# 184 groups of mixer steps of a three-block transformer kernel take another place among the weight slots, by a table

## The chip, the core and the metric

The kernel runs on one core of a Trainium2 chip. The metric is the device time of one execution in microseconds (us), the median of three runs. The engines are named as in the profile: PE is TensorE (matmuls) and PEld its weight loads, DVE is VectorE, ACT is ScalarE, POOL is GpSimd, and SP is the engine that issues the DMAs.

## What is computed

Three blocks follow each other on one sequence of 256 tokens of 2048 numbers, in fp32. The first joins an RWKV-7 mixer and a chunked attention, the second a top-k sparse attention and a spatial gate, the third a pooling mixer and a dilated attention; the second and third end in a squared-relu MLP.

```python
def first_block(x, ...):
    h = _rms_norm(x, pre_norm_g)
    p_r, p_k, p_v, z_r, q_a, k_a_att, v_a, z_a, m_r, m_a = split(h @ w_in)
    y_r = _rwkv7_mixer(h, p_r, p_k, p_v, ...) * silu(z_r)
    y_a = _chunk_band_attention(q_a, k_a_att, v_a, rel_bias) * silu(z_a)
    merged = (sigmoid(m_r + b_merge[0]) * (y_r @ w_branch_rwkv)
              + sigmoid(m_a + b_merge[1]) * (y_a @ w_branch_attn))
    return x + _rms_norm(merged @ w_out, post_norm_g)

def second_block(x, ...):
    q, k, v, qi, ki, wi, u_s, v_s, ga, gb = split(rms_norm(x, norm1_g) @ w_in)
    attn = sparse_attention(q, k, v, qi, ki, wi, rel_bias)
    sgu = spatial_gating(gelu(u_s), gelu(v_s), sgu_ln_g, sgu_ln_b, sgu_w, sgu_b)
    x = x + (sigmoid(ga) * attn + sigmoid(gb) * sgu) @ w_out
    x = x + square(relu(rms_norm(x, norm2_g) @ w_ff1)) @ w_ff2
    return rms_norm(x, final_g)

def third_block(x, ...):
    u, q, k, v = split(rmsnorm(x, norm_mix_g) @ w_in)
    y_pool = rmsnorm(pool_mixer(u, pool_w, pool_scale), pool_out_norm_g)
    y_attn = rmsnorm(dilated_attention(q, k, v, slopes), attn_out_norm_g)
    x = x + concatenate([y_pool, y_attn]) @ w_out
    x = x + square(relu(rmsnorm(x, norm_mlp_g) @ w_up)) @ w_down
    return rmsnorm(x, norm_final_g)
```

## The kernel before

**The weight stream.** All large products run in one stream of 1084 slots. A slot is eight blocks of 128 weight rows by 128 columns. For each pair of slots SP loads 1 MB into a ring of three (`load_unit`, L2419). For each slot ACT copies the weights to a rounded high half (`split_high`, L2429), DVE subtracts it to get the low half (`split_low`, L2436), and PE multiplies: eight matmuls of the high half with the token operand's two halves (128x512, L2526) and eight of the low half (128x256, L2530), all into a sums buffer `gp`. The splits run two slots ahead of PE, in four slots' worth of `w_parts`. When a block of columns ends, its sums are read out by ACT (L2037), DVE (L2139, L2143, L2177) and in some sections POOL (L2081).

The sections follow each other in this order, with the first slot of each: `qkv` 0, `za` 48, `rkv` 64, `gates` 112, `zr` 176, `branch` 192, `out` 224 (block 1); `index2` 256, `qkv2` 268, `v2` 316, `u2` 348, `ga2` 380, `gb2` 412, `out2` 444, `up2_0` 476, `down2_0` 540, `up2_1` 604, `down2_1` 668 (block 2); `in3` 732, `out3p` 796, `out3a` 812, `up3_0` 828, `down3_0` 892, `up3_1` 956, `down3_1` 1020 (block 3, to 1084).

**The steps beside it.** Everything else (the mixers, attentions, norms, tables) is written as "threads". A `Thread` has a start place, counted in slots, a pace, and one generator for each engine that works for it; each `yield tick` gives the place `start + tick * pace` of what follows. A `Beside` object on each engine's instruction stream runs the steps whose place has been reached. PE asks it at the start of a slot (q), after half of the high products (q + 0.34) and after all of them (q + 0.67); ACT and DVE ask at the same three places, `side.run(q)` standing ahead of the slot's `split_high` or `split_low`, the other two behind it and around the read-out of a block. The engines run in order, so a step whose inputs are late holds back whatever stands behind it on its engine. Data and waits are fixed by semaphores; only the order on each engine follows from the places.

**Names that the prediction uses.** Threads `rwkv_0` and `rwkv_1` work each on four groups of heads, one after another (0 to 3), beside `gates` and `zr`. Of one group: `norms` (DVE L963 and L965 give `kk_squared`, PE L1115 sums it over a head: `headones`), `norm_spread` (after the root chain on DVE, L969 then L90 to L95, then L975; PE L1115 with `ident,smalls`), `cumulated` (DVE L997 sigmoid, PE L1115 with `consts`, then three exponentials on ACT, L1082 to L1084), `ab`/`ak` (DVE L1004 to L1009 `r_hat`, `z_hat`, `b_hat`, `k_hat`, then PE L1115 64x128), and at the group's end `mean`, `var`, the same root chain and `var_spread` (L1055, L90 to L95, then PE and DVE L1062). All PE steps of these threads go through one helper, L1115. Threads `att2_0`, `att2_1` (beside `qkv2` to `gb2`) and `att3_0`, `att3_1` (beside `in3`) are attentions: DVE stages v, k and q (L1293, L1294, L1299, into `low`), PE transposes v (L1348) and makes logits (L1354, L1355), ACT copies (L1329), and later PE transposes the probabilities (L1361). `sgu_0`/`sgu_1` are the spatial gate (DVE L1660, PE L1692). `pool` is the pooling mixer beside `in3` (its last DVE step is L1809), `tables3` makes distance tables beside `up2_0` (DVE L1737 to L1744), `start` and `lora` stand at the beginning (norms of x: PE L419 waits for a DVE root chain ending in L95), and `post` between `out` and `index2`.

Of the kernel before, what the change touches and what calls it, by code (L numbers as in the profile page):

```python
# [34 lines left out]
FAR, TAKEN = -1.0e38, -3.0e38  # L35


class Section:


    def __init__(self, name, blocks, nk, source, wide=False):
        self.name, self.blocks, self.nk, self.source, self.wide = name, blocks, nk, source, wide
        self.chunks = SLOT // 2 if wide else SLOT
        self.slots = nk // self.chunks
        self.slot0 = self.block0 = 0
# [14 lines left out]
class Beside:  # L60


    def __init__(self, eng, key, threads):
        self.live = []
        for t in threads:
            if key in t.programs:
                g = t.programs[key](eng)
                self.live.append([t, g, next(g, None)])

    def run(self, place):  # L70
        for entry in self.live:
            t, g, tick = entry
            while tick is not None and t.start + tick * t.pace <= place + 1e-9:
                tick = next(g, None)
            entry[2] = tick


class InverseRoot:
# [2530 lines left out]
```

## Time and profile before

| | us |
|---|---|
| median of three runs | 3455.51 (3454.36 to 3463.07) |
| span of the profiled execution | 3455.6 |
| PE busy | 3366.9 (97%) |
| PE weight loads busy | 2908.9 (84%) |
| DVE busy | 2204.8 (64%) |
| ACT busy | 1543.8 (45%) |
| POOL busy | 295.2 (9%) |

The span runs from the first to the last instruction of the profiled execution, which is the only one for which a trace exists; it is within 0.1 us of the median of the three. PE busy is the share of the span in which a matmul was in work, the weight loads overlap it, and a busy PE is not PE at its full rate: the same matmul takes about twice as long where the granted clock is at its lower level.

### The profile page before, as it was taken

How to read it: one execution, taken by the hardware profiler on the slowest of the kernel's cores; microseconds unless marked ns; L12 is line 12 of the kernel's file. 1: busy time of each engine (PE TensorE's matmuls, PEld its weight loads, DVE VectorE, ACT ScalarE, POOL GpSimd, SP SyncE). 2: the span in 40 equal slices, each digit the busy share in tenths (PEclk: the TensorE clock that was granted, in tenths of full speed). 3: DMA queues.
4: the chain of work that ended last, by engine and by line, in shares of the span. 5: the costliest groups of instructions: out<-in, count | busy, mean ns of one | idle time of the engine just before them, and what ended most of it. 6: DMA issues, size and time to landing. Idle time of an engine off the chain costs nothing.

```text
span 3455.6 us, 52015 instructions
## 1 busy us (share of the span) xinstructions
PE 3366.9 (97%) x21718; PEld 2908.9 (84%) x21718; DVE 2204.8 (64%) x3040; ACT 1543.8 (45%) x2121; POOL 295.2 (9%) x318
## 2 busy tenths in 40 slices
PE   8999999999989999999999999999999999999998
PEld 7888877778878888888888888888888888888887
DVE  5567655556667576777666446655777866446654
ACT  4454433334543455544544334444454544334443
POOL 3100122220011111100100000001000100000000
PEclk9999999999989999999999999999999999999999
DMA  6554433335535545655555656555544556556554
GB/s 193 180 178 151 138 111 116 107 107 195 190 123 171 187 154 169 193 164 173 182 193 186 193 185 192 187 191 188 166 159 159 183 184 207 194 183 195 192 198 146
DMA packets 550751, 592.98 MB, mean 172 GB/s; under 512 B 16757, under 2 KB 511733, under 8 KB 550262
## 3 DMA queue, kind: packets, MB, share of 16 engines
q1 hardware_dynamic: 550518, 589.66, 52.7%
q8 instruction: 172, 2.82, 0.3%
q14 instruction: 61, 0.50, 0.0%
HBM read 583.24 MB, written 6.32 MB: 171 GB/s over the span
## 4 chain that ended last, share of the span: by engine, by line
PE 87%; DVE 7%; ACT 2%; issue 2%; DMA 1%; POOL 0%; SPq 0%; DVEq 0%; ACTq 0%; POOLq 0%
PE gp L2526 45%; PE gp L2530 24%; PE gp L2511 7%; PE sidep L1115 4%; PE gp L2516 3%; DVE w_parts L2436 2%; ACT w_parts L2429 1%; DVE stage L2143 0%; DMA high<-bias_rows 0%; PE sidep L570 0%; ACT lo_half L2037 0%; PE sidep L1355 0%; DVE stage L2139 0%; DMA ring<-w_branch_rwkv 0%; DVE low L2175 0%
## 5 line engine op out<-in xcount | busy, mean ns | idle before, releaser
L2436 DVE TENSOR_TENSOR w_parts<-ring,w_parts 128x1024 fp32r<-128x1024 f32 x1084 | 1368.9, 1285 | 452.8 <-ACT w_parts L2429 451.5
L2526 PE MATMUL gp<-x_parts,w_parts 128*128 128x512 f32 x5840 | 1481.7, 398 | 11.1 <-issue 5.5
L2429 ACT ACTIVATE w_parts<-ring 128x1024 fp32r<-128x1024 f32 x1084 | 1109.8, 1053 | 453.5 <-PE gp L2516 188.9
L2526 PEld LDWEIGHTS gp<-x_parts,w_parts 128*128 128x128 f32 x5840 | 1061.7, 190 | 215.6 <-issue 13.4
L2530 PEld LDWEIGHTS gp<-x_parts,w_parts 128*128 128x128 f32 x5840 | 771.8, 191 | 48.0 <-issue 6.7
L2530 PE MATMUL gp<-x_parts,w_parts 128*128 128x256 f32 x5840 | 801.4, 285 | 2.8 <-DVE w_parts L2436 2.6
L2037 ACT ACTIVATE lo_half<-gp 128x512 f32<-128x512 f32 x239 | 142.8, 598 | 892.1 <-PE gp L2526 459.4
L2526 PE MATMUL gp<-ff_parts,w_parts 128*128 128x512 f32 x1792 | 430.8, 391 | 0.0
L2526 PEld LDWEIGHTS gp<-ff_parts,w_parts 128*128 128x128 f32 x1792 | 328.6, 188 | 63.0
L2139 DVE TENSOR_TENSOR stage<-gp,lo_half 128x512 f32<-128x512 f32 x168 | 116.2, 692 | 377.3 <-ACT lo_half L2037 376.4
L2511 PE MATMUL gp<-w_parts,ff_parts 128*128 128x512 f32 x1024 | 273.7, 389 | 0.0
L2530 PEld LDWEIGHTS gp<-ff_parts,w_parts 128*128 128x128 f32 x1792 | 230.9, 191 | 10.6 <-issue 1.4
L2530 PE MATMUL gp<-ff_parts,w_parts 128*128 128x256 f32 x1792 | 235.4, 283 | 0.3 <-DVE w_parts L2436 0.3
L2511 PEld LDWEIGHTS gp<-w_parts,ff_parts 128*128 128x128 f32 x1024 | 192.3, 188 | 39.9
L538 POOL TENSOR_TENSOR low<-low 128x512 f32<-128x512 f32 (+1 forms) x38 | 59.0, 1558 | 1237.0 <-ACT low L529 648.9
L2516 PE MATMUL gp<-w_parts,ff_parts 128*128 128x512 f32 x512 | 157.5, 389 | 0.0
L2139 DVE TENSOR_TENSOR high<-gp,lo_half 128x512 f32<-128x512 f32 x63 | 43.5, 691 | 165.8 <-ACT lo_half L2037 165.7
L2053 ACT ACTIVATE ff_parts<-stage 128x512 fp32r<-128x512 f32 x64 | 40.5, 632 | 166.8 <-DVE stage L2177 166.8
L2516 PEld LDWEIGHTS gp<-w_parts,ff_parts 128*128 128x128 f32 x512 | 96.1, 188 | 19.9
L2081 POOL TENSOR_TENSOR high<-high,rstd 128x512 f32<-128x512 f32 x40 | 57.5, 1437 | 458.5 <-DVE high L2139 440.7
L1115 PEld LDWEIGHTS sidep<-high 64*64 64x64 f32 x1696 | 60.3, 133 | 42.7 <-issue 17.8
L1115 PE MATMUL sidep<-high 64*64 64x64 f32 (+1 forms) x1696 | 73.4, 233 | 16.2 <-DVE high L1007 4.6
(392 smaller groups left out, 1867.1 us busy)
## 6 DMA issues: line engine op xcount, KB each, us to landing
ring<-w_in SPq DMA_DIRECT2D x220, 1024.0 KB, 5.1
ring<-w_ff SPq DMA_DIRECT2D x128, 1024.0 KB, 5.6
ring<-w_up SPq DMA_DIRECT2D x64, 1024.0 KB, 6.0
ring<-w_down SPq DMA_DIRECT2D x64, 1024.0 KB, 5.0
ring<-w_out SPq DMA_DIRECT2D x48, 1024.0 KB, 5.3
ring<-w_branch_attn SPq DMA_DIRECT2D x8, 1024.0 KB, 5.2
ring<-w_branch_rwkv SPq DMA_DIRECT2D x8, 1024.0 KB, 5.2
gate_scratch<-stage SPq DMA_DIRECT2D x16, 256.0 KB, 2.2
```

The costliest lines, as they stand in the source:

```text
L538: m = pool.tensor_tensor(self.acc[k], self.acc[k], self.sq[b - 1][k], ALU.add)
L1115: return pe.matmul(out, lhs, rhs, start=start, stop=stop, skip_group_check=True)
L2037: act.activation(lo_half[:, k % 2], gp[:, k % 2, :, 1, :], ACT.Copy).then_inc(lo_copied, 1)
L2053: act.activation(ff_parts[:, 2 * b:2 * b + 2, 0, :], st, ACT.Copy).then_inc(ff_high_split, 1)
L2081: pool.tensor_tensor(to, to, over(rstd, 2), ALU.mult).then_inc(scaled_by_pool, 1)
L2139: v.tensor_tensor(to, gp[:, k % 2, :, 0, :], lo_half[:, k % 2], ALU.add).then_inc(block_evacuated, 1)
L2429: act.activation(w_parts[:, q % PARTS, 0], ring[:, u % RING, SLOT * (q % 2):SLOT * (q % 2) + SLOT, :], ACT.Copy).then_inc(high_split, 1)
L2436: v.tensor_tensor(w_parts[:, q % PARTS, 1], ring[:, u % RING, SLOT * (q % 2):SLOT * (q % 2) + SLOT, :], w_parts[:, q % PARTS, 0].bitcast(F ...
L2511: pe.matmul(wide_sums(k, t), operand(s, b, s.chunks * n + c)[:, half, tokens], w[:, 0, c, :], start=(n == 0 and c == 0 and half == 0), sto ...
L2516: m = pe.matmul(wide_sums(k, t), operand(s, b, s.chunks * n + c)[:, 0, tokens], w[:, 1, c, :], start=False, stop=(n == s.slots - 1 and c = ...
L2526: return pe.matmul(gp[:, k % 2, j, :, :], w_parts[:, q % PARTS, 0, c, j * P:(j + 1) * P], operand(s, b, SLOT * n + c), start=(n == 0 and c ...
L2530: return pe.matmul(gp[:, k % 2, j, 0, :], w_parts[:, q % PARTS, 1, c, j * P:(j + 1) * P], operand(s, b, SLOT * n + c)[:, 0, :], start=Fals ...
```

## The change

A table `MOVED` gives, for a thread and an engine, the number of slots that are added to the place of its n-th step (counted from 0); `Beside` adds it when it asks whether a step has been reached. Most steps have no entry and stay. The table has 185 entries: 105 on PE, 64 on VectorE, 15 on ScalarE (these are the 184 of the title) and one on SyncE, a load of a table; 105 make the step later, 80 earlier. No instruction, wait or buffer is added or taken away. Line numbers after the table are 58 higher in the changed kernel (L1115 is L1173 there).

```diff
+MOVED = {
+    ("att2_0", "tensor"): {0: 1.12, 1: 0.57, 7: 0.7, 13: 1.29, 14: 1.07, 20: 0.87},
...
+    ("att3_1", "vector"): {0: -0.16, 14: -0.5},
...
+    ("pool", "vector"): {15: 1.17},
...
+    ("rwkv_0", "tensor"): {0: 1.72, 1: 0.88, 30: 0.35, 31: -0.1, 32: -0.05, 35: -0.18, 38: -0.2, 39: -0.09, 40: -0.32,
+        42: -0.1, 49: -0.36, 50: -0.58, 51: -0.48, 55: -0.05, 56: -0.28, 61: 0.42, 62: 1.47, 63: 1.63, 66: 0.44,
+        92: -0.01, 115: -0.01, 116: -0.24, 117: -0.46, 121: 1.12},
...
+    ("tables3", "vector"): {0: -2},
...
+}
@@ class Beside
-                self.live.append([t, g, next(g, None)])
+                self.live.append([t, g, next(g, None), 0, MOVED.get((t.name, key), {})])
 
     def run(self, place):
         for entry in self.live:
-            t, g, tick = entry
-            while tick is not None and t.start + tick * t.pace <= place + 1e-9:
-                tick = next(g, None)
-            entry[2] = tick
+            t, g, tick, n, moved = entry
+            while tick is not None and t.start + tick * t.pace + moved.get(n, 0) <= place + 1e-9:
+                tick, n = next(g, None), n + 1
+            entry[2:4] = tick, n
```

What it does to the order is shown at three places. The first is PE at the start of `v2` (block 2), where the two attention threads begin a group: L1348 transposes v, L1354 and L1355 make the logits. Before:

```order
L2530 MATMUL gp<-x_parts,w_parts 128x256 x8
L2526 MATMUL gp<-x_parts,w_parts 128x512 x8
L1348 MATMUL sidep<-ident,low 128x128 x4
L2530 MATMUL gp<-x_parts,w_parts 128x256 x8
L2526 MATMUL gp<-x_parts,w_parts 128x512 x4
L1354 MATMUL sidep<-low 128x128
L1355 MATMUL sidep<-low 128x256
L1354 MATMUL sidep<-low 128x128
L1355 MATMUL sidep<-low 128x256
L2526 MATMUL gp<-x_parts,w_parts 128x512 x4
```

and after, from one slot further on:

```order
L2588 MATMUL gp<-x_parts,w_parts 128x256 x8
L2584 MATMUL gp<-x_parts,w_parts 128x512 x8
L1406 MATMUL sidep<-ident,low 128x128 x2
L1412 MATMUL sidep<-low 128x128
L1413 MATMUL sidep<-low 128x256
L2588 MATMUL gp<-x_parts,w_parts 128x256 x8
L2584 MATMUL gp<-x_parts,w_parts 128x512 x4
L1406 MATMUL sidep<-ident,low 128x128 x2
L2584 MATMUL gp<-x_parts,w_parts 128x512 x4
L1412 MATMUL sidep<-low 128x128
L1413 MATMUL sidep<-low 128x256
```

The transposes moved more than a slot later and the two threads' are apart now; the first thread's logits follow its transposes at once.

The second is DVE beside `in3` (block 3), where the pooling mixer's last step, L1809, stands near the staging of the dilated attention (L1293, L1294, L1299). Before:

```order
L2436 TENSOR_TENSOR w_parts<-ring,w_parts 128x1024
L2143 TENSOR_TENSOR high<-high,rstd 128x512
L1809 SCALAR_TENSOR_TENSOR ff_parts<-high,prm,ff_parts 128x256 x8
L594 COPY variance_t<-sidep 128x256
L1293 TENSOR_SCALAR low<-high 128x256
L1294 TENSOR_SCALAR low<-high 128x256
L1299 TENSOR_SCALAR low<-high 128x256
L2436 TENSOR_TENSOR w_parts<-ring,w_parts 128x1024
```

and after:

```order
L652 COPY variance_t<-sidep 128x256
L1351 TENSOR_SCALAR low<-high 128x256
L1352 TENSOR_SCALAR low<-high 128x256
L1357 TENSOR_SCALAR low<-high 128x256
L2494 TENSOR_TENSOR w_parts<-ring,w_parts 128x1024
L1351 TENSOR_SCALAR low<-high 128x256
L1352 TENSOR_SCALAR low<-high 128x256
L1357 TENSOR_SCALAR low<-high 128x256
L1867 SCALAR_TENSOR_TENSOR ff_parts<-high,prm,ff_parts 128x256 x8
```

The eight instructions of L1809 (L1867 now) stand behind the staging of both attention threads instead of ahead of it.

The third is PE beside `gates` (block 1), about slot 154, where the third group of the RWKV heads gets its running sums (`consts,high` is thread 0, `consts,low` thread 1) and then its `ab`/`ak` products (64x128, both threads). Before:

```order
L1115 MATMUL sidep<-consts,high 128x256 x2
L1115 MATMUL sidep<-consts,low 128x256 x2
L2526 MATMUL gp<-x_parts,w_parts 128x512 x4
L2530 MATMUL gp<-x_parts,w_parts 128x256 x8
L2526 MATMUL gp<-x_parts,w_parts 128x512 x8
L1115 MATMUL sidep<-high 64x128 x32
```

and after:

```order
L1173 MATMUL sidep<-consts,low 128x256 x2
L2584 MATMUL gp<-x_parts,w_parts 128x512 x4
L1173 MATMUL sidep<-consts,high 128x256 x2
L1173 MATMUL sidep<-high 64x128 x32
L2588 MATMUL gp<-x_parts,w_parts 128x256 x8
```

The sums of thread 0 moved about a slot later, and now stand directly ahead of the products that need what ACT and DVE make of them. In the other groups (0, 1 and 3) the sums moved later by a third to a half of a slot, and of group 3 the `ab`/`ak` products too.

## Rows read from the trace of the kernel before

**Rows 1.** The page: its busy times, and the chain that ended last.

```profile
PE 3366.9 (97%) x21718; PEld 2908.9 (84%) x21718; DVE 2204.8 (64%) x3040; ACT 1543.8 (45%) x2121; POOL 295.2 (9%) x318
...
PE 87%; DVE 7%; ACT 2%; issue 2%; DMA 1%; POOL 0%; SPq 0%; DVEq 0%; ACTq 0%; POOLq 0%
```

**Rows 2.** PE by stretches: from:to us, length, busy (xcount), granted clock, DMA share, GB/s.

```profile
391.70:741.70 350.00, 327.32 (x4326) 1.00 0.34 111
741.70:818.10 76.40, 70.29 (x831) 0.98 0.32 104
...
1009.60:1052.80 43.20, 39.99 (x197) 0.82 0.23 64
...
1198.70:1313.80 115.10, 109.20 (x635) 0.97 0.53 167
...
1888.20:2423.90 535.70, 535.70 (x3073) 1.00 0.60 190
```

**Rows 3.** PE's waits, whole span: waiting line, awaited line: us in total, times, longest.

```profile
PE sidep L1348 <- DVE low L1293: 7.0, 5, 2.4
...
PE sidep L419 <- DVE smalls L95: 5.9, 3, 2.6
...
PE sidep L1115 <- DVE high L997: 5.5, 4, 1.6
PE sidep L1115 <- DVE high L1007: 4.6, 2, 3.4
...
PE sidep L1115 <- DVE high L965: 3.4, 2, 2.5
PE sidep L1692 <- DVE low L1660: 3.1, 5, 1.2
...
PE sidep L1354 <- DVE low L1299: 2.5, 2, 1.3
...
PE sidep L1361 <- DVE low L1314: 2.4, 4, 1.0
```

**Rows 4.** Timeline, end of `gates`, group 3: start, duration, engine, line, operation [idle before].

```profile
712.63 1.30 PE L2530 MATMUL gp<-x_parts,w_parts 128*128 128x256 f32 x8
...
714.46 0.47 ACT L1082 ACTIVATE high<-sidep,consts 128x256 f32<-128x256 f32 x1
...
715.60 1.11 PE L2530 MATMUL gp<-x_parts,w_parts 128*128 128x256 f32 x8
...
719.67 0.42 DVE L1007 TENSOR_TENSOR high<-high 128x256 f32<-128x256 f32 x1
...
720.14 1.09 PE L1115 MATMUL sidep<-high 64*64 64x128 f32 x16 [3.43 <-DVE high L1007]
```

**Rows 5.** Timeline, a root chain at the start of `gates`: its first and last instruction.

```profile
400.51 0.22 DVE L969 TENSOR_SCALAR smalls<-sidep 128x4 f32<-128x4 f32 x2
...
404.44 0.17 DVE L975 TENSOR_SCALAR smalls<-smalls 128x8 f32<-128x8 f32 x1
```

**Rows 6.** Timeline, `zr`: PE's spread step behind a root chain.

```profile
807.02 1.97 PE L1115 MATMUL sidep<-ident,smalls 128*64 128x128 f32 x16 [2.37 <-DVE smalls L95]
```

**Rows 7.** Timeline, start of `v2`: the first thread's transposes.

```profile
1211.07 0.44 PE L1348 MATMUL sidep<-ident,low 128*128 128x128 f32 x2 [1.97 <-DVE low L1293]
```

**Rows 8.** Timeline, `in3`: the pooling mixer's last step, and the transposes behind it.

```profile
2522.09 3.26 DVE L1809 SCALAR_TENSOR_TENSOR ff_parts<-high,prm,ff_parts 128x256 fp32r<-128x256 f32 x8
...
2526.06 0.44 PE L1348 MATMUL sidep<-ident,low 128*128 128x128 f32 x2 [2.37 <-DVE low L1293]
```

**Rows 9.** Timeline, `up2_0`: the table chain's first instruction, and PE behind it.

```profile
1735.61 0.29 DVE L1737 CAST consts<-variance_t 128x256 f32<-128x256 int32 x1
...
1740.65 1.18 PE L2530 MATMUL gp<-x_parts,w_parts 128*128 128x256 f32 x8 [2.19 <-DVE w_parts L2436]
```

**Rows 10.** PE behind the waits of Rows 4 and 7, columns as in Rows 2.

```profile
720.10:741.70 21.60, 21.56 (x405) 1.00 0.30 100
...
1213.20:1216.60 3.40, 3.40 (x14) 0.50 0.37 92
```

More of the change, by code:

```diff
@@ L35 @@
 FAR, TAKEN = -1.0e38, -3.0e38
+MOVED = {
+    ("aout_rms", "tensor"): {1: 0.67},
+    ("att1_0", "tensor"): {2: 1.24, 4: 1.2, 5: 1.17, 8: 1.04, 14: 0.5, 16: 0.47},
+    ("att1_1", "tensor"): {2: 1.24, 5: 1.17, 8: 1.04, 14: 1.5},
+    ("att2_0", "scalar"): {5: 0.72},
+    ("att2_0", "tensor"): {0: 1.12, 1: 0.57, 7: 0.7, 13: 1.29, 14: 1.07, 20: 0.87},
+    ("att2_0", "vector"): {2: -0.3, 9: 0.82, 16: 1.17},
+    ("att2_1", "scalar"): {9: 0.74},
+    ("att2_1", "sync"): {1: -0.5},
+    ("att2_1", "tensor"): {0: 1.79, 1: 1.57, 2: 0.39, 6: 0.35, 7: 0.37, 13: 0.95, 14: 0.74, 15: 0.55, 20: 0.54},
+    ("att2_1", "vector"): {8: -0.08, 24: -0.25},
+    ("att3_0", "tensor"): {2: 0.47},
+    ("att3_1", "tensor"): {2: 0.97, 6: 0.64, 10: 1.3, 11: 0.44},
+    ("att3_1", "vector"): {0: -0.16, 14: -0.5},
+    ("bias2", "vector"): {0: 0.84},
+    ("gelu_u", "scalar"): {0: 1.66},
+    ("lora", "tensor"): {1: 0.84, 2: 0.67},
+    ("lora", "vector"): {5: 0.34, 6: 0.5},
+    ("merged", "scalar"): {0: 1},
+    ("merged", "vector"): {0: 1},
+    ("mlp3", "tensor"): {0: 0.33, 1: 0.34},
+    ("mlp3", "vector"): {1: -0.66},
+    ("norm1", "tensor"): {0: 1.33, 1: 2},
+    ("norm2", "tensor"): {0: 0.33, 1: 0.34},
+    ("pool", "vector"): {15: 1.17},
+    ("post", "scalar"): {1: 1.34, 2: 2.66, 3: 2.33},
+    ("post", "vector"): {1: -0.34},
[13 rows of a table added]
+    ("select", "vector"): {15: 0.67, 16: 1.17, 17: 3},
+    ("sgu", "scalar"): {2: 0.79, 3: 1.12},
+    ("sgu", "tensor"): {1: 2.17, 2: 0.67},
+    ("sgu", "vector"): {9: 0.67, 10: 0.79},
[4 rows of a table added]
+    ("start", "tensor"): {5: -1.33, 6: -0.33, 7: -0.67, 8: -1, 9: -2.36},
+    ("start", "vector"): {5: -1.02, 6: -1, 7: 0.68},
+    ("tables3", "vector"): {0: -2},
+    ("y_a", "vector"): {0: -0.67},
+    ("y_r", "scalar"): {1: 1},
+    ("y_r", "vector"): {1: 1.33},
+    ("ya", "scalar"): {6: -1},
+}
 class Section:
```

14 rows, old and new, of the table MOVED are left out of this document.

## The prediction, made before the changed kernel was run

> **What bounds the kernel now.** I read the page first. PE is busy for 3366.9 us of 3455.6, and the chain that ended last is PE for 87% [rows 1]. So PE's stream sets the end, and an edit is worth only what it takes from PE: idle time, time at the lower clock, or matmuls that run slowly. The reader should see next that the busy share flatters PE: on the same page the weight loads are busy for 84% only. The Trainium skill says so too (Perfetto Trace Analysis, "Identifying the Most-Contended Engine"): matmul busy time is a poor measure and the weight loads a better one. The sum below doesn't use that; it goes by waits.
>
> Second, PE by stretches. PE idles 3455.6 - 3366.9 = 88.7 us. The MLP of block 2 has none: 535.70 us of 535.70 [rows 2], and at 16 matmuls a slot its 3073 are 192 slots, so a slot is 2.79 us of PE. `gates` has 350.00 - 327.32 = 22.7, `zr` 6.1, the index section 3.2, `v2` 5.9 [rows 2]: it sits where mixer steps lie in the stream. The largest piece I know of outside the table's reach is the transition to block 2 around `post` and the load of x at the start; together with the tail they are about half of the 88.7.
>
> Third, the waits, by what PE stood for [rows 3]. All the large ones have one form: a mixer step on PE reached before DVE had its operand ready. There a later place for PE's step costs nothing and takes the wait away, since weight products of later slots are ready in between. Fourth, the clock: 3.40 us at a granted clock of 0.50 [rows 10] is the lower of its two levels (1.2 instead of 2.4 GHz), so it does 1.7 us of work and loses 1.7. There are nine places with such stretches; the shown one begins 2.1 us after the end of a wait of 1.97 [rows 7].
>
> **The change, part by part.** Nothing is added or removed, so the only terms are waits that go, waits that come, the clock behind them, and detours: each time PE leaves the stream and returns, the first group of weight products takes 1.30 us instead of 1.11 [rows 4], so 0.19 each.
>
> *Start and `lora`.* PE's L419 waited 2.6 of its 5.9 us here for the root chain [rows 3]; its step is put 2.7 slots later. The transposes of x are pulled into the time in which PE waits for the first split anyway. Together 2.6 and an estimated 1.4 from the transposes: **4.0**.
>
> *`gates`, what goes.* The running sums (waiting for L997) are later in groups 0, 1 and 3, and in group 2 for one thread: 5.5 us [rows 3]. The `ab`/`ak` products of group 3 move on by 1.3 to 1.6 slots, that is at least 3.6 us of stream, against a wait of 3.43 [rows 4]; the shorter wait for L1007 goes too except for a few tenths, 4.2 of 4.6 [rows 3]. Of the other 22.7 - 5.5 - 4.6 - 3.4 = 9.2 us, which are waits of 0.4 to 1.9 for level products, states and sums, the table moves PE's side later or DVE's side earlier at about half: 4.9.
>
> *`gates`, what comes.* (a) Group 0's norm sums are later by 1.5 slots, so the 3.4 us for L965 go [rows 3]. But the spread of the roots now has the same place, and stands directly behind the second sum. It needs the root chain, 404.44 + 0.17 - 400.51 = 4.1 us [rows 5], or some 2.4 without POOL beside it, by PE's wait of 2.37 for most of such a chain in `zr` [rows 6]. PE will wait about 3.1 there: net +0.3. (b) In group 2 the sums of thread 0 are directly ahead of the products made from them. Between stand three exponentials and three DVE operations, 3 x 0.47 + 3 x 0.42 = 2.7 [rows 4], and no weight product: a new wait of 2.7. (c) The spread of group 0's deviations is earlier by a half slot or so than its chain: 1.1. Sum for `gates`: 5.5 + 4.2 + 4.9 + 0.3 - 2.7 - 1.1 = **11**.
>
> *`zr`.* All idle time there is waits of this form, 2.37 of it for one root chain [rows 6]. That spread is later by 1.1 slots, more than 3 us. A stretch at the lower clock follows it at once. 6.1 + 1.7, less seven detours more (1.3): **6.5**.
>
> *The attentions and the spatial gate, `v2` to `gb2`.* L1348 waited 7.0 us, 2.37 of it in `in3` [rows 3, 8], so 4.6 here; L1354 2.5 and L1692 3.1 [rows 3]. L1348 is later by 1.12 slots and 1.79 slots for the two threads, 3.1 us and more against 1.97 [rows 7]; for L1692 PE's steps are later by 0.5 to 1. Two stretches at the lower clock stand behind the L1348 waits: 2 x 1.7. Together 10.2 + 3.4, and 0.9 of smaller waits: **14.5**.
>
> *Index section.* Its wait for the second half of the operand is 2.9 of its 3.2 idle [rows 2]; a `post` step on DVE is earlier by a third and ACT's are later, out of the way: **2.0**, an estimate between 0 and 2.9.
>
> *`up2_0`.* The table chain begins at 1735.61, and PE waits 2.19 for the split behind it, until 1740.65 [rows 9]; less about 1.2 for that split the chain is some 3.8 us of DVE. It goes two slots back, behind that slot's splits. What is late next is the split after it, which is two slots ahead of PE (5.6 us) against 3.8 of chain: covered. **2.2**.
>
> *`in3`, `out3p`.* L1809 is 3.26 us of DVE ahead of the staging for which PE waited 2.37 [rows 8]. Behind both stagings it delays one `split_low` only, which is two slots early. So 2.4, one lower clock stretch 1.7, L1361's 2.4 [rows 3] and 0.9 for the norm there (L419): **7.4**.
>
> *The rest* (`rkv`, `branch`, `qkv2`, `up3_0`): **1.7**.
>
> Gross 4.0 + 11 + 6.5 + 14.5 + 2.0 + 2.2 + 7.4 + 1.7 = 49.3. Against it: PE has 15 detours more, of which I counted seven, 8 x 0.19 = 1.5. And waits that the trace of before can't show, since a step that moves brings its followers to an edge: I set one of 0.5 us for each of 11 later steps that are at a following step's place, 5.5; the bounds are nothing and 1.5 us each (the middle of the waits above), 16. The sum is 49.3 - 1.5 - 5.5 = 42, on 3455.5: **3413**. The profiled execution's 3455.6 and the median 3455.51 agree, so no scaling.
>
> **Does the clock come back?** The sum takes back four slow stretches (one in `zr`, two behind L1348, one in `in3`), 4 x 1.7 = 6.8 us. It is the least sure term: after a wait of 3.43 [rows 4] the granted clock is 1.00 for the 21.6 us behind it, while after 1.97 [rows 7] it falls [rows 10]. A fifth, at the start of `gates`, I leave where it is, since the wait there stays. The Trainium skill's rule (TensorE: Matmul & The Clock Gate, "HAM oscillation") has it that a kernel whose PE pauses for its operands is given the lower clock for the work behind. By that the pauses' end ends these stretches, 6.8 us; if they come regardless of the pauses, the sum is 35 and the time 3420.
>
> **The rivals.**
> 1. *The waits come back elsewhere.* The root chains and exponentials are as long as before; if PE reaches the following step too early, half of what was saved returns, as I found at (a), (b) and (c), where 7 of 21 us return. At half, 21 us are left: 3435. For it: in `gates` almost every step has a follower within a slot or two. Against it: in `v2` and `in3` a group's steps are spread wide.
> 2. *All that is named goes, new waits don't come,* and (a) to (c) are shorter than worked out (PE reaches them later, and DVE is ahead): 49.3 + 7 = 56: 3399.
> 3. *Slower: a DVE side step blocks a split.* 45 or so of the 64 VectorE entries are earlier. One whose input isn't there holds DVE, and with it `split_low` behind it. It costs what [rows 9] shows, 2.19 us, once the hold exceeds the two slots' lead (5.6 us less the split, 1.2). To turn 42 us of gain into no change it takes 42 / 2.2, about 19 such places; at 25 it is 3468. It speaks against it that DVE has 36% of the span free, and that the earlier ones move by a quarter to a half slot (0.7 to 1.4 us), less than the lead.
> 4. *It doesn't do what it says:* steps are reached only at three places a slot, so an entry may round to the old place. The order shows otherwise on PE (three places in the section on the change). Then 3455.
>
> **How the numbers follow.** The forecast 0.63 (own range 3404 to 3424), rival 1 0.17, rival 2 0.11, rival 3 0.05, rival 4 0.04. The predicted time is the forecast's, 3413. Its bounds from the unseen waits are 49.3 - 1.5 - 16 = 32 and 48, so 3424 and 3408; the clock term adds 7 above. The range has to take in most of rivals 1 and 2: 3396 to 3437. A measurement of this kernel can tell about 0.3%, 10 us, from no change: faster means below 3445. Faster: the forecast, rival 2 and all but a little of rival 1, 0.90. Within 0.3%: rival 4 and what is left of rival 1 and the small end of rival 3, 0.06. Slower: 0.04.
>
> **What would show it.** PE idle from 88.7 to about 50. In `gates` from 22.7 to about 12; two waits of PE's L1173 of about 3 us remain or are new there, one at its start for a root chain (its spread), one about slot 154 for L1065. No wait of 2 us at the start of `v2`, in `in3`, in `zr`, nor behind the table chain in `up2_0`, and full clock behind each. The MLPs take the same 535.7. It would be wrong if waits of `w_parts` L2494 appear at PE (rival 3), or if PE's idle time falls while its busy time rises by as much, which would be detours dearer than 0.19 or matmuls slowed otherwise.

## The result, and the profile after

The changed kernel took 3396.92 us (3396.3 to 3398.74, four runs) against 3457.82 for the kernel before (3454.36 to 3463.07), a ratio of 0.9821 with a 95% interval of 0.9807 to 0.9835. It is faster by 60.9 us where 42 were forecast. On the kernel before's 3455.5, from which the prediction was worked out, the ratio gives 3393.7, below the stated range that began at 3396 (the 3396.92 itself lies just inside it, but beside a kernel before of 3457.82). So the direction was right and the size too small by a third.

The page of the changed kernel (span 3394.6 us), the lines that answer to [rows 1]:

```profile
PE 3350.2 (99%) x21718; PEld 2901.7 (85%) x21718; DVE 2199.1 (65%) x3040; ACT 1541.8 (45%) x2121; POOL 305.4 (9%) x318
...
PE 95%; DVE 3%; issue 1%; DMA 0%; POOL 0%; ACT 0%; SPq 0%; DVEq 0%; ACTq 0%; POOLq 0%
```

VectorE's part of the chain that ended last fell from 7% to 3%. PE idles 3394.6 - 3350.2 = 44.4 us, 44.3 less than before. But its busy time fell as well, by 16.7, for the same 21718 matmuls, where the prediction took 6.8 off for the clock and added 2.8 for detours. PE by stretches, as [rows 2] (`gates`, `zr`, index section, `v2`, the MLP of block 2):

```profile
385.00:721.50 336.50, 328.54 (x4325) 0.98 0.35 115
721.50:791.50 70.00, 69.70 (x833) 1.00 0.35 114
...
982.50:1022.00 39.50, 36.76 (x196) 0.90 0.24 67
...
1168.00:1271.30 103.30, 103.30 (x625) 1.00 0.58 182
...
1838.00:2373.70 535.70, 535.70 (x3074) 1.00 0.60 190
```

`v2` has no idle time left (5.9 us before), `zr` 0.3 of 6.1, `gates` 8.0 of 22.7. The MLP is the same to 0.1 us. Of the waits of [rows 3] those for L1293, L997, L965, L1660, L1299 and L1314 are gone altogether. Apart from the first 20 us and from DMA and split waits, the largest for a VectorE step that are left are these; L1173 is the L1115 of before, L1033 its L975, L1065 its L1007, L153 its L95:

```profile
PE sidep L1173 <- DVE smalls L1033: 4.1, 1, 4.1
PE sidep L1173 <- DVE high L1065: 2.4, 1, 2.4
PE sidep L477 <- DVE smalls L153: 2.4, 1, 2.4
...
PE sidep L1173 <- DVE smalls L153: 1.1, 1, 1.1
```

The first, second and fourth are the prediction's (a), (b) and (c): 3.1, 2.7 and 1.1 us forecast. The third is at the transition to block 2, where it is 2.4 before as well. Two waits are new at the very start: 1.9 for a load of x, in place of 2.7 for the first split, and 0.7 for L748.

In us, stage by stage. "Clock" is half the change of the time spent at a granted clock of 0.5 (the last 540 us, equally long in both, are left out of it); the last column is what neither idle time nor clock explains:

| stage | forecast | measured | idle | clock | rest |
|---|---|---|---|---|---|
| start, `qkv` | -4.0 | -3.6 | -2.9 | -0.9 | +0.2 |
| `rkv`, `branch`, `qkv2`, `up3_0` | -1.7 | -4.0 | -1.6 | 0 | -2.4 |
| `gates` | -11 | -13.5 | -14.7 | +3.4 | -2.2 |
| `zr` | -6.5 | -6.4 | -5.8 | -1.7 | +1.1 |
| index section | -2.0 | -3.7 | -0.5 | -3.9 | +0.7 |
| `v2` to `gb2` | -14.5 | -17.4 | -11.3 | -3.4 | -2.6 |
| `up2_0` | -2.2 | -2.4 | -2.2 | 0 | -0.2 |
| `in3`, `out3p` | -7.4 | -10.2 | -5.7 | -3.4 | -1.1 |
| whole span | -42 | -61.0 | -44.3 | -9.4 | -7.3 |

(The forecast's total has 7 us taken off for detours and unseen waits; its stages add up to 49.)

The clock of the first row is not what the clock records alone give. They begin at 18.5 us in the kernel before and at 10.9 in the changed one, and a stretch without a record counts as full clock. The kernel before's first weight products, then the changed kernel's:

```profile
13.37 2.04 PE L2526 MATMUL gp<-x_parts,w_parts 128*128 128x512 f32 x4 [2.66 <-ACT w_parts L2429]
...
15.92 2.05 PE L2526 MATMUL gp<-x_parts,w_parts 128*128 128x512 f32 x4
```

```profile
13.25 1.17 PE L2584 MATMUL gp<-x_parts,w_parts 128*128 128x512 f32 x4
```

The first take nearly twice as long for the same work, so the 5.1 us from 13.4 to 18.5 are counted as the lower level here, against the 3.4 recorded in the changed kernel. That is an inference from the durations.

### The profile page after: what moved, and what is told of

Its sections match the earlier page's. It is cut to its first block, busy times and chain, and to the rows that moved or that the text cites. A ratio compares the mean times of both kernels' runs of the same rounds, so it can differ in the third digit from the quotient of the medians.

```text
span 3394.6 us, 52013 instructions
## 1 busy us (share of the span) xinstructions
PE 3350.2 (99%) x21718; PEld 2901.7 (85%) x21718; DVE 2199.1 (65%) x3040; ACT 1541.8 (45%) x2121; POOL 305.4 (9%) x318
## 4 chain that ended last, share of the span: by engine, by line
PE 95%; DVE 3%; issue 1%; DMA 0%; POOL 0%; ACT 0%; SPq 0%; DVEq 0%; ACTq 0%; POOLq 0%
PE gp L2584 50%; PE gp L2588 26%; PE gp L2569 7%; PE sidep L1173 4%; PE gp L2574 3%; DVE w_parts L2494 1%; PE sidep L1413 0%; PE sidep L628 0%; PE sidep L1498 0%; PE sidep L1419 0%; POOL high L596 0%; PE sidep L1757 0%; PE sidep L900 0%; PE sidep L1879 0%; PE sidep L764 0%
## 5 line engine op out<-in xcount | busy, mean ns | idle before, releaser
L2584 PEld LDWEIGHTS gp<-x_parts,w_parts 128*128 128x128 f32 x5840 | 1058.4, 189 | 211.2 <-issue 10.9
L2588 PEld LDWEIGHTS gp<-ff_parts,w_parts 128*128 128x128 f32 x1792 | 230.9, 191 | 10.9 <-issue 1.8
L1173 PEld LDWEIGHTS sidep<-high 64*64 64x64 f32 x1696 | 60.5, 133 | 30.1 <-issue 17.9
L2139 POOL TENSOR_TENSOR stage<-stage,rstd 128x512 f32<-128x512 f32 x32 | 49.6, 1549 | 350.0 <-DVE stage L2197 350.0
```

The lines of the kernel that those rows point to most:

```text
L1173: return pe.matmul(out, lhs, rhs, start=start, stop=stop, skip_group_check=True)
L2139: pool.tensor_tensor(to, to, over(rstd, 2), ALU.mult).then_inc(scaled_by_pool, 1)
L2584: return pe.matmul(gp[:, k % 2, j, :, :], w_parts[:, q % PARTS, 0, c, j * P:(j + 1) * P], operand(s, b, SLOT * n + c), start=(n == 0 and c ...
L2588: return pe.matmul(gp[:, k % 2, j, 0, :], w_parts[:, q % PARTS, 1, c, j * P:(j + 1) * P], operand(s, b, SLOT * n + c)[:, 0, :], start=Fals ...
```

## What a wait costs beside PE's idle time

A source of the last column stands in the timeline. Two places of the same step, the three transposes L1361 in `in3`; first the kernel before, where PE waited for VectorE:

```profile
2541.02 1.10 PE L2530 MATMUL gp<-x_parts,w_parts 128*128 128x256 f32 x8
...
2542.16 0.35 DVE L1314 TENSOR_SCALAR low<-low,smalls 128x256 f32<-128x256 f32 x1
...
2542.56 0.31 PEld L1361 LDWEIGHTS sidep<-ident,low 128*128 128x128 f32 x3 [0.64 <-DVE low L1314]
2542.56 0.55 PE L1361 MATMUL sidep<-ident,low 128*128 128x128 f32 x3 [0.44 <-DVE low L1314]
...
2542.86 1.41 PE L2526 MATMUL gp<-x_parts,w_parts 128*128 128x512 f32 x5
```

and the changed kernel, where the operand is ready (L1419 is L1361):

```profile
2523.22 1.09 PE L2584 MATMUL gp<-x_parts,w_parts 128*128 128x512 f32 x4
...
2523.41 0.35 DVE L1372 TENSOR_SCALAR low<-low,smalls 128x256 f32<-128x256 f32 x1
...
2523.92 0.48 PEld L1419 LDWEIGHTS sidep<-ident,low 128*128 128x128 f32 x3
2524.15 0.49 PE L1419 MATMUL sidep<-ident,low 128*128 128x128 f32 x3
...
2524.40 1.17 PE L2584 MATMUL gp<-x_parts,w_parts 128*128 128x512 f32 x4
```

Without a wait the weight load begins 0.23 us ahead of its first matmul, beneath the matmul before it. With a wait both begin at once. Count from the moment at which the stream's next product could have begun, one product's interval (0.12 us for 256 columns, 0.23 for 512) behind the start of the last: the detour takes 0.90 us with the wait and 0.25 without, 0.65 for 0.44 of idle time. The same reading at other waits of the kernel before whose step has one form: L1348 in `in3` 2.58 for 2.37, L1692 five times 0.21 to 0.23 more than its idle time, L1354 1.54 for 1.26, L419 2.81 for 2.57. So each of these waits costs PE's idle entry and another 0.21 to 0.28 us. It isn't so for every wait: L1440, which waits for a DMA, costs 0.03 more.

Where the 0.21 of L1361 lies can be read from the single records. The last product starts at 2541.84 and its modelled end is 2542.12, so the idle entry begins 0.16 behind 2541.96, when the next could have started: matmuls in a row overlap, and the entry leaves that out. The other 0.05 is the first transpose, 0.33 us instead of the 0.27 of the next, with its load now ahead of it. Whether the other waits divide in this way was not read.

A test without the clock: e9 below leaves block 2 as it was, and has no lower clock in `v2` and `u2`, like the changed kernel. They take 215.6 us there and 206.4 in the changed kernel. Of the 9.2 us 7.5 are idle time; the other 1.7 come with seven waits, 0.24 each.

PE's list of waits has 57 before and 18 now. 39 x 0.25 is 9.8, an estimate that is above the 7.3 of the last column; the 15 detours more can be the difference, and so can the halving of the slow time, which is too much in `zr` and the index section, where the last column is positive. Neither is shown. The rows on which the prediction stood hinted at the price: [rows 7, 8] are PE's entries, and the idle entry of PEld is nearer to it, 0.64 for 0.65 at L1361 and 2.79 for 2.58 at L1348.

## Experiments

All but the three shifted ones are the table with other entries; the line numbers of an experiment are up to 51 above those of before. e5 to e11 and e14 ran once each: they are read stage by stage, from their traces, and not by their totals.

### Which side of the table does it?

The first takes PE's entries alone, the second all others.

```diff
 MOVED = {
     ("att1_0", "tensor"): {...},
-    ("att2_0", "scalar"): {...},
-    ("att2_0", "vector"): {...},
...
```

> The changed kernel with only the 105 PE entries of the table; VectorE, ScalarE and SyncE keep their places. Theory A (the gain of about 61 us is PE reaching its mixer steps later, when their operands are ready): at least 50 of the 61 us come, about 3400 to 3408; missing are the L1809 wait in in3 (2.4 and a slow stretch), the table chain in up2_0 (2.2) and the index section (3.7). Theory B (the two sides have to be shifted together; a DVE step at its old place ahead of a split now waits for a PE step that is later, and holds the split): less than 35 us come, 3420 or more, and PE waits for w_parts L2494.

Measured: 3454.76 us (3450.54 to 3456.6), ratio 0.9984 (0.9974 to 0.9993). Theory A, which is also the prediction's, falls: 4 us, not 50. PE in `gates`, then its waits there:

```profile
386.90:755.60 368.70, 339.25 (x4326) 0.96 0.32 105
```

```profile
PE sidep L1136 <- DVE high L1028: 7.0, 3, 3.4
PE sidep L1136 <- DVE high L1054: 4.3, 2, 3.7
PE sidep L1136 <- DVE smalls L996: 3.9, 1, 3.9
PE sidep L1136 <- DVE high L1018: 3.4, 3, 1.5
PE sidep L1136 <- DVE high L1000: 3.2, 1, 3.2
```

`gates` is 368.7 us long instead of 350.0: PE idles 29.5 instead of 22.7 there, and 30.6 us of it run at the lower clock instead of 3.4, which costs 13.7 by halving. `v2` shows the table's other face: it is shorter by 8.8 of the 11.8 us. The total is theory B's, but its sign, waits for the split, is hardly there: PE waits 4.0 us for VectorE's `w_parts` in all, 2.9 before. What PE waits for is the mixer's own operands.

> The changed kernel with only the 80 entries of VectorE, ScalarE and SyncE; PE keeps its places. Theory A: about 8 to 12 us faster than before (in3 4.1, up2_0 2.2, index section 3.7, little in gates), 3444 to 3448. Theory B: the earlier VectorE steps alone shorten many of the waits in gates and zr, 20 us or more in all, 3435 or less.

Measured: 3443.9 (3441.59 to 3444.72), ratio 0.9952 (0.9937 to 0.9967). The two halves give 4 and 15 us, together 19 of the 61. Neither theory: `in3`, `out3p` and `up2_0` gave 9.6 as A had it, and the early steps of VectorE 3.6 in `gates` (6.5 of idle time, half of which the lower clock took back: 10.2 us of it instead of 3.4) and 2.4 in `zr`, as B had it, but new waits came where VectorE's side had been moved later without PE's:

```profile
PE sidep L1382 <- DVE low L1327: 6.0, 3, 3.2
PE sidep L1601 <- DVE low L1627: 4.0, 1, 4.0
PE sidep L1388 <- DVE low L1333: 3.0, 2, 1.5
```

These are L1348 (4.6 before), L1567 (0.8) and L1354 (2.5), between `v2` and `gb2`. In the index section PE waits 4.0 us for POOL's operand, 0.3 before, as in e8 below.

The third leaves out, of PE's entries, the 27 that make a step earlier.

```diff
-    ("rwkv_0", "tensor"): {0: 1.72, 1: 0.88, 30: 0.35, 31: -0.1, 32: -0.05, 35: -0.18, ...
+    ("rwkv_0", "tensor"): {0: 1.72, 1: 0.88, 30: 0.35, 61: 0.42, 62: 1.47, 63: 1.63, 66: 0.44, 121: 1.12},
```

> Of the table only PE's 78 entries that make a step later; its 27 earlier ones and all of VectorE, ScalarE and SyncE are left out. If the earlier PE steps spoiled e1 (they need operands that VectorE makes no earlier), gates has less idle time than the 29.5 us of e1 and of the 22.7 of before: 17 us or less, and the kernel is at 3435 to 3445. If PE's later steps themselves hold VectorE and thereby the next step, gates idles 25 us or more again, and the kernel is at 3450 or above.

Measured: 3443.44 (3440.69 to 3447.75), ratio 0.9955 (0.9939 to 0.9972). The time is the first theory's, the place is not. PE's earlier steps did cost e1 some 10 us (ratios 0.9984 and 0.9955), but in `gates` the later ones by themselves save nothing:

```profile
387.80:744.60 356.80, 333.58 (x4326) 0.98 0.34 109
```

23.2 us of idle time against 22.7, which is neither the 17 or less of the first theory nor the 25 or more of the second; the stage is 6.8 us longer than before by the clock, 17.1 us at the lower level instead of 3.4. Where the waits of the kernel before went, others came: L995 (L975 before) has 3.9, L1027 (L1007) 7.0 in three places instead of 4.6 in two. The reading that fits: a PE step that is later makes what VectorE and ScalarE do with its result later too, and if the following PE step stays, it waits. The table moves both sides.

### The step that the prediction told wrongly

The prediction put the waits of 1.63 and 3.43 us in the last group of heads [rows 4] down to a later place of PE's steps there, and so does the section on the change, in its last sentence. The table has no such entry: in groups 0, 1 and 3 PE's sums stay where they are, behind as many weight products as before (2744 in group 3), and so do the `ab`/`ak` products of group 3. What is moved there is VectorE, and one step of ScalarE.

```diff
+    ("rwkv_0", "vector"): {69: -0.24, 70: -0.46, 71: -1.02, 72: -0.2},
+    ("rwkv_1", "vector"): {69: -0.24, 70: -0.46, 71: -1.02},
+    ("rwkv_0", "scalar"): {43: -0.13},
```

> The kernel before with eight entries only: of group 3 of rwkv_0 and rwkv_1 the VectorE steps sigmoid, kka and hats are earlier by 0.2 to 1.0 slots, one ScalarE step by 0.13; no PE step moves. It tells apart who took away the waits of 1.63 (L997, at 711.0) and 3.43 us (L1007, at 720.1). The prediction put them down to a later PE step; the table has no such entry for group 3. Theory B (VectorE's earlier steps do it): both waits go, the idle time of gates falls from 22.7 to about 17.6. Rival (PE's later steps do it): both stay.

PE's waits in `gates` for the same two lines, L1004 (L997) and L1014 (L1007):

```profile
PE sidep L1122 <- DVE high L1004: 3.9, 3, 1.6
...
PE sidep L1122 <- DVE high L1014: 1.1, 1, 1.1
```

One of four and one of two are gone, 1.6 and 3.5 us; the idle time of `gates` is 346.00 - 328.48 = 17.5. So these eight entries bring the 5 us without any PE step. In the trace VectorE's sigmoid comes earlier and its products stand ahead of a `split_low` (L2436) instead of behind it; and the one ScalarE entry puts the first thread's exponentials (L1082) ahead of a read-out (L2037), 1.07 us behind the start of the sums instead of 3.47. Which of the two the wait for L1007 needed was not taken apart. This is shown for group 3.

### Single places

> The kernel before with nine entries of the table only: PE's transposes and logits (L1348, L1354) of att2_0 and att2_1 at the starts of both groups are later by 0.6 to 1.8 slots. The waits 1.97, 0.92, 0.85 and 0.91 us go, 4.6 us. Theory A (the slow stretches at 1213.2 and 1308.7 come from the pauses ahead of them): they go too, 3.4 us more, so v2 shrinks from 115.1 to 107 or less. Rival (they come from something else, or by chance): both stay, v2 is 110.5.

```diff
+    ("att2_0", "tensor"): {0: 1.12, 1: 0.57, 13: 1.29, 14: 1.07},
+    ("att2_1", "tensor"): {0: 1.79, 1: 1.57, 13: 0.95, 14: 0.74, 15: 0.55},
```

`v2`, as in [rows 2], and what PE still waits for in it:

```profile
1207.90:1316.40 108.50, 104.25 (x625) 1.00 0.53 170
```

```profile
PE sidep L1354 <- DVE low L1299: 1.6, 1, 1.6
PE sidep L1367 <- DVE low L1320: 1.4, 2, 1.0
PE sidep L1360 <- DVE low L1305: 1.3, 1, 1.3
```

115.1 became 108.5. Both stretches at the lower clock are gone from it (0.97 became 1.00), as theory A has it, but that doesn't show theory A: e9, with the same waits in `v2` as before (5.9 us), has neither stretch either and takes 112.0, and e3, e7 and e8, which leave these waits alone, have one. Against e9 the edit gives 3.5 us. Of idle time 1.6 us are gone: the start of the first group no longer waits, while the transposes of the second wait 1.6 at one place instead of 0.85 and 0.91 at two, and the probabilities' transposes (L1367, the L1361 of before) wait 1.4 that wasn't there. The other entries of these threads take those away in the changed kernel. The run as a whole took 3461.36, no less than before, because `gates`, which the edit doesn't touch, was 7.5 us longer. The next section is on that.

> The kernel before with one entry: the pooling mixer's last VectorE step (eight instructions, 3.26 us) is 1.17 slots later, behind the staging of both attention threads. The wait of 2.37 for L1293 goes, and by theory A the slow stretch behind it (1.7): in3 from 213.1 to 209.0. If the held split or the next attention step takes the place of that wait, 211 to 213.

```diff
+    ("pool", "vector"): {15: 1.17},
```

`in3` became 210.4 us, 2.7 less. The wait of 2.37 for the first transposes is gone and another of 1.3 has come, so the idle time fell by 1.0, which is nearer to the rival's case. The other 1.7 are the stretch at the lower clock behind it, and they aren't the edit's: e3, e6, e8 and e9 keep the wait, lack the stretch and take 211.4 or 211.5.

```profile
PE sidep L1353 <- DVE low L1298: 1.3, 1, 1.3
```

> The kernel before with the four entries of the thread post: ScalarE's roundings of x for block 2 (groups 1 to 3) are later by 1.34, 2.66 and 2.33 slots, and a VectorE step is earlier by 0.34. The index section took 43.2 us before and 39.5 in the changed kernel. Theory A: these four entries give at least 3 of the 3.7 us (40.2 or less), with the wait for L2295 shorter. Rival: most of the 3.7 us is a slow stretch less, which comes or goes with the timing of what precedes: 42 or more here.

The index section became 44.7 us, 1.5 longer. Its wait for the operand's second half fell, but the step ahead now waits for POOL:

```profile
PE sidep L576 <- POOL high L544: 2.9, 1, 2.9
PE gp L2532 <- DVE x_parts L2301: 1.8, 2, 0.9
```

In the changed kernel `norm1`'s steps on PE are 1.33 and 2 slots later as well, and that wait is 0.4. Of the 3.7 us there, 3.9 are the clock, and the clock isn't the table's alone: e4 below has the same entries here, 13.3 us at the lower level instead of 8.0, and takes 41.2.

> Only the entries of the threads rwkv_0 and rwkv_1, on all engines (87 of 185). If stages are independent: gates 336.5 us long as in the changed kernel (350.0 before), zr 70.0 (76.4 before), all other stages as before: 19.9 us less, 3436. If what one stage gives the next (DMA prefetch, slow stretches carried over) counts, the sum differs by more than 2 us.

Measured: 3436.97 (3433.29 to 3437.04), ratio 0.9931 (0.9916 to 0.9945). `gates` and `zr`:

```profile
392.00:728.40 336.40, 328.41 (x4325) 0.98 0.35 115
728.40:798.30 69.90, 69.60 (x832) 1.00 0.36 114
```

That is the changed kernel's 336.5 and 70.0. The entries of this mixer work on their own stages and can be tuned by themselves; e1, e2 and e13 show that PE's and the other engines' can't be taken apart within `gates`.

### The price of a detour

```diff
+    ("att1_1", "tensor"): {0: 0.34, 1: 0.34, ...},
```

> The kernel before, with one entry set that the change doesn't have: all 24 PE steps of the thread att1_1 (beside rkv) get 0.34 slots, so that they no longer stand directly behind those of att1_0. PE leaves the weight stream 18 times more. By the prediction's price of 0.19 us per detour the stage rkv grows from 172.6 us by 3.4, less up to 1.4 of waits that a later place removes: 174.6 or more. Rival: a detour costs nothing of its own, since weight products of the stream fill what the step's own chain leaves open: 171.2 to 172.6.

```profile
219.10:393.10 174.00, 172.91 (x994) 1.00 0.48 158
```

The stage took 174.0 us, 1.4 more than before, for 18 detours more; 0.4 us of waits went, so 0.10 each, between the 0.19 expected and the rival's nothing. It hangs on the step: pairs of L834, L841 and L842 took 2.38 us together and 1.17 + 1.16 apart, L858 to L860 1.54 and then 0.89 + 0.90. The prediction's 0.19, read off the longer first group of products behind a detour [rows 4], is thus too dear here. What the 15 more detours cost in the changed kernel can't be told from the price of its waits.

### The clock

Before and the same kernel with a shift:

```diff
                         pe.wait_ge(high_split, q + 1)
+                        for _ in range(4 if s.name == "za" and b == 1 and n == 0 else 0):
+                            high_product(0, 0)
```

> The kernel before with four matmuls more (the first product of a block in za is made five times, each time started anew; 128x512, 0.228 us each), so that everything behind slot 52 comes 0.9 us later and nothing else changes. Theory C (whether a pause brings a slow stretch hangs on when it falls, so the same program has another set of them when it is shifted): gates to in3 show slow stretches at other places than before, and the time differs from before plus 0.9 by several times 1.7 us, up or down. Rival (slow stretches belong to their pauses): the same nine places, each 0.9 later, and 3456.5.

> As e10 with eight matmuls more, a shift of 1.8 us. Theory C: a third set of slow stretches, other than those of before and of e10. Rival: the same places, 1.8 later, and 3457.4.

They took 3465.14 and 3463.34, beside 3460.61 (3454.35 to 3466.3, seven runs) for the kernel before in the same comparison. Four stretches of the kernel with the shift of 0.9 us, in `gates` and `zr`:

```profile
503.80:507.20 3.40, 3.40 (x14) 0.50 0.20 77
677.90:681.30 3.40, 3.40 (x8) 0.51 0.20 77
725.60:729.00 3.40, 3.40 (x38) 0.51 0.17 43
793.90:797.30 3.40, 3.40 (x33) 0.50 0.00 0
```

and the same work in the kernel before, found by counting weight products (0.9, 2.6, 4.3 and 6.0 us earlier, since each slow stretch on the way delays what follows by another 1.7):

```profile
502.90:506.30 3.40, 3.40 (x30) 1.00 0.20 77
675.30:678.70 3.40, 3.40 (x49) 1.00 0.20 77
721.30:724.70 3.40, 3.40 (x52) 1.00 0.18 49
787.90:791.30 3.40, 3.40 (x53) 1.00 0.00 1
```

The waits in `gates` and `zr` are the same, the clock is not: 14 matmuls in place of 30 at the first. `gates` idles 22.7 us in both and takes 354.8 instead of 350.0. Shifted by 1.8, there are slow stretches at 505.2 and 573.4 in `gates`, and one in `branch` at 856.7, with those at 677.9 and 725.6 gone. Theory C holds: the same pause on PE may or may not be followed by one, and a shift of 0.9 us changes which. The seven runs of the kernel before in that comparison show it without a shift; span and mean granted clock:

```
3452.6 us 0.992    3453.7 us 0.992    3457.0 us 0.991    3458.9 us 0.990
3459.7 us 0.990    3459.4 us 0.989    3464.5 us 0.988
```

The profiled execution on which the prediction rests (3455.6 us, 0.992) was among the quick ones. So was its `gates`: of the seven traces in which the table leaves that stage alone (the kernel before, e5 to e8, e10, e11) it idles 22.1 to 22.7 us in all, and takes 350.0 to 357.5, with 3.4 us at the lower clock in the kernel before and 20.5 in e6. The stage table above, which sets one execution against one, is uncertain by as much in its clock column. The same shift on the changed kernel:

> The changed kernel with four matmuls more in za, a shift of 0.9 us as in e10. If slow stretches need pauses, and it has few, its set stays small: 3396.3 + 0.9, within 3.4, and no stretch between slots 120 and 255. If they come by chance regardless of pauses, new ones appear in gates to gb2 and it is 3 to 8 us longer.

It took 3396.24 us, and its span, 3394.5, is the changed kernel's 3394.6: `gates` took 336.1 for 336.5, and the rest of the 0.9 us lies in a few tenths elsewhere. One slow stretch did come within it, at 604.9 behind the wait for L1065, in the place of one at the start of `gates`, so the set isn't fixed (none was expected there), but it stays as small. Outside the transition to block 2 and the last 540 us the four kernels with all or nearly all of the table (the changed one, e4, e12, e14) have 7 to 17 us of recorded lower clock, those of the seven traces above 24 to 44. The changed kernel's four runs lie within 2.4 us, where the kernel before's four had 8.7; but e12's four spread over 6.1, so a small spread isn't shown to be the table's.

### Can the table be bettered?

Each of these alters a few entries at the waits (a), (b) and (c).

```diff
-    ("rwkv_0", "tensor"): {..., 63: 1.63, ...}
+    ("rwkv_0", "tensor"): {..., 63: 1.3, ...}
```

> The changed kernel with one entry altered: in rwkv_0 on PE, step 63 (the running sums of group 2) is later by 1.30 instead of 1.63 slots, so it stands beside that of rwkv_1 and half of a slot's high products lie between it and the ab/ak products. The changed kernel waits 2.42 us there. 0.9 us of matmuls now lie between: the wait falls to about 1.3 and one detour less: 1.1 to 1.5 us faster than the changed kernel, 3395.5, ratio to before 0.9817. Rival: DVE holds the split first and the exponentials come no earlier: no change, 3397.

Measured: 3395.4 (3394.47 to 3395.68), ratio 0.9819 (0.9803 to 0.9835). The wait is 1.2 us instead of 2.4. The second has this, and in both threads on PE `1: 1.22, 2: 0.43, 31: 0.16`:

> The changed kernel with e4's edit and six more entries altered: at the start of gates PE's spread of the norm roots is a third of a slot later (115.34) for both threads and the step behind it another third (115.67); at slot 133 the spread of group 0's deviations is a third later. Half of a slot's products (0.9 us) then lie under each of the waits of 4.06 and 1.05 us: 4.06 falls to 3.1 or less, 1.05 to 0.1 or less. About 1.5 to 1.9 us less than e4 (3395.4): 3393.7, unless the next step waits instead, in which case 3395.4.

Measured: 3394.65 (3390.35 to 3396.45), ratio 0.9809 (0.979 to 0.9828). PE's waits in `gates`:

```profile
PE sidep L1166 <- DVE smalls L1026: 3.0, 1, 3.0
PE sidep L1166 <- DVE high L1058: 1.2, 1, 1.2
PE sidep L1166 <- DVE high L1084: 0.3, 1, 0.3
```

4.1, 2.4 and 1.1 became 3.0, 1.2 and nothing, as expected; that the whole gained 1.5 us or more beyond e4, as was expected too, isn't shown. The medians are 1.5 and 2.3 us below the changed kernel's, but the intervals of the ratios lie over each other: the waits are shown to be shorter, that the kernel is faster is not.

## Why the prediction was right or wrong

- **What bounds the kernel** was right. PE sets the end, the gain is waits in the mixer stages, and the MLPs didn't change.
- **The idle time** came out near what was named: 49.3 gross, without its 6.8 of clock and with the 1.3 taken off for detours in `zr`, is 43.8, and 44.3 were measured. `zr` was right to a tenth in sum; (b) was 2.42 for 2.7, (c) 1.05 for 1.1, (a) 4.06 for 3.1: the root chain took 4.0 us there, with POOL busy beside all of it.
- **"... the only terms are waits that go, waits that come, the clock behind them, and detours": the largest miss.** A wait was priced at PE's idle entry and its further price put at nothing. At the waits that could be read it is 0.21 to 0.28 us more. What neither idle time nor clock explains came out at -7.3 where the forecast, which had only detours there, had +2.8: 10.1 us of the 18.7 by which the measured 61.0 exceeds the forecast's 42.3. The term was partly to be read in PEld's idle time, and the prediction itself had said that PE's busy share flatters.
- **The term of 5.5 for unseen waits:** wrong. Idle time fell by 44.3 where the forecast had 38.3 with this term, 6.0 of the 18.7. New waits of more than half a microsecond are the three found from the order and two at the start (1.9, in place of 2.7, and 0.7). **Detours at 0.19:** 0.10 in e5, and not to be told apart in the changed kernel.
- **"There a later place for PE's step costs nothing and takes the wait away":** wrong for `gates`. Alone, later PE steps save nothing there (23.2 us of idle time), PE's entries in both directions lose 18.7 us, and in group 3 it is VectorE's and ScalarE's steps that do it. The total for `gates` was near because both sides are in the table; the reason given for half of it was not the one.
- **The clock:** 9.4 us instead of 6.8, the last 2.6 of the 18.7. The four stretches that were named went. Besides, `gates` has two more (+3.4), the index section, the start of `in3` and the first products have less (-3.9, -1.7, -0.9); the index section's is what took it 1.7 us past its term. That the four went because their pauses did isn't shown: e9 lacks both of `v2`, and e3, e6, e8 and e9 that of `in3`, with the pauses in place. The rule of the Trainium skill (TensorE: Matmul & The Clock Gate, "HAM oscillation") that a kernel whose PE pauses is given the lower clock behind the pauses agrees with the traces taken together, 24 to 44 us with all or most of the pauses and 7 to 17 without most of them, and none in the MLP of block 2, which has no pause; the shifted kernels show that no single pause can be counted on to bring one.
- **The rivals.** Half coming back: no, though e1 shows how near it lies, for one side of the same table gains nothing. All gone and no new waits (3399): the nearest, and still above the result, for want of the wait's full price and of some clock. A split blocked by VectorE: PE waits 0.9 us for it in the changed kernel, 2.9 before.

## What to carry to other kernels

Price a wait of TensorE above the idle entry of its matmuls: here it cost 0.2 to 0.3 us more at nearly every wait that was read. The idle entry of its weight loads is nearer. When steps of several engines are interleaved by a table, move both ends of a dependency together and judge a stage as a whole, since either end alone gave 0.2 and 0.5 of the 1.8 per cent. And take several executions before you count stretches at a lower clock: which pauses bring them changed with a shift of 0.9 us.

## What was not expected of the hardware

Four and eight matmuls more, 0.9 and 1.8 us of work, made the profiled span 7.8 and 6.1 us longer, mostly by the lower clock granted at other places. The waits in `gates` and `zr` were the same; in `v2` L1348 waited 1.2 and 1.1 us more, and with eight matmuls PE also waited 1.8 more for a split.

And the first clock record of a trace can come late, at 18.5 us in the kernel before, though its products from 13.4 us on ran at about half their rate. So e6, with two recorded stretches of 3.4 us in `qkv` where the kernel before has none, has 6.8 us at the lower level there against 5.1, and that the stage took 174.9 us for 174.5 doesn't show that a slow stretch at the start is cheap.
